# Scan on the vector engine, gates among the value steps, lag kernels before the indexer tile, column quarters and key turns within the value tiles

## What is computed

```
P = rms_norm(h) @ w_in       # u_s5 512 | q 512 | k 512 | v 512 | q_idx 256, k_idx 32, w_idx 8 | gate_s5, gate_att 1024 each
# branch S5: 32 groups of 16 channels, 64 complex states per group
s_t = a * s_(t-1) + B u_t    # diagonal, complex, over the sequence
y   = Re(C s_t) + D u_t      # then GELU and a GLU
# branch DSA
I[t,s] = sum_h w[t,h] relu(q_idx[t,h] . k_idx[s])
keep the top k (128 of the prompt, 256 of the past of a sample); softmax attention over them,
with a relative bias; the samples read k and v from a paged cache by a page table
h = h + (sigmoid(gate_s5) * S5 + sigmoid(gate_att) * DSA) @ w_out
```

## Time and profile before

| | us |
|---|---|
| median of 3 runs (1504.95 to 1506.29) | 1506.16 |
| the profiled execution, its own time | 1504.8 |
| its span | 1503.1 |
| busy: PE / DVE / ACT / POOL | 1425.5 / 609.4 / 451.4 / 262.3 |
| granted clock of PE, mean | 0.979 |

### The profile page before, as it was taken

How to read it: one execution, slowest core, us unless ns; L and a number is a source line. 1 busy time by engine, 2 the same in 40 slices (tenths; PEclk the granted TensorE clock), 3 DMA queues, 4 the chain that set the end, 5 groups by cost and what they waited for, 6 DMA issues and landing times. The chain is left out here.

```text
span 1503.1 us, 27575 instructions
## 1 busy us (share of the span) xinstructions
PE 1425.5 (95%) x10734; PEld 1294.4 (86%) x10734; DVE 609.4 (41%) x957; ACT 451.4 (30%) x647; POOL 262.3 (17%) x458
## 2 busy tenths in 40 slices
PE   6999999999999989989999897989999999999996
PEld 5999999999977767767777774848999999999996
DVE  4333233434452267506666321205543443344344
ACT  4332222222330320145555331202332212221234
POOL 4000000487002109701134313110000000000000
PEclk8999999999998999999999999999999999999998
DMA  8522332232222472153211658661233223322221
GB/s 135 153 84 77 87 89 84 85 90 86 63 56 34 99 115 60 24 137 75 57 57 57 196 179 300 195 224 42 84 88 94 85 84 87 95 85 84 83 71 60
DMA packets 228746, 148.05 MB, mean 98 GB/s; under 512 B 29729, under 2 KB 211817, under 8 KB 228666
## 3 DMA queue, kind: packets, MB, share of 16 engines
q1 hardware_dynamic: 195904, 118.06, 27.1%
q0 software_dynamic: 7088, 19.65, 5.3%
q10 hardware_dynamic: 25674, 9.25, 3.4%
HBM read 139.62 MB, written 6.12 MB: 97 GB/s over the span
## 5 line engine op out<-in xcount | busy, mean ns | idle before, releaser
L1614 DVE TENSOR_TENSOR w_low<-wraw,w_high 128x1024 fp32r<-128x1024 f32 x144 | 180.4, 1254 | 318.8 <-ACT w_high L1141 318.8
L575 PE MATMUL ps<-hn_high,w_high 128*128 128x272 f32 x1408 | 292.4, 289 | 2.9 <-DVE w_low L1614 2.9
L575 PE MATMUL ps<-hn_high,w_low 128*128 128x272 f32 x1408 | 292.4, 289 | 0.0
L575 PE MATMUL ps<-hn_low,w_high 128*128 128x272 f32 x1408 | 291.3, 288 | 0.0
L1141 ACT ACTIVATE w_high<-wraw 128x1024 fp32r<-128x1024 f32 x144 | 152.5, 1060 | 443.0 <-PE ps L575 437.9
L575 PEld LDWEIGHTS ps<-hn_high,w_high 128*128 128x128 f32 x1408 | 222.4, 189 | 3.1 <-issue 3.0
L575 PEld LDWEIGHTS ps<-hn_low,w_high 128*128 128x128 f32 x1408 | 222.2, 189 | 0.0
L575 PEld LDWEIGHTS ps<-hn_high,w_low 128*128 128x128 f32 x1408 | 220.7, 190 | 0.0
L575 PE MATMUL ps<-act_high,w_high 128*128 128x272 f32 x832 | 173.1, 289 | 3.0 <-DVE act_low L1614 1.8
L575 PE MATMUL ps<-act_high,w_low 128*128 128x272 f32 x832 | 172.2, 288 | 0.0
L575 PE MATMUL ps<-act_low,w_high 128*128 128x272 f32 x832 | 171.6, 288 | 0.0
(11 more groups left out here) (328 smaller groups left out, 1591.8 us busy)
## 6 DMA issues: line engine op xcount, KB each, us to landing
wraw<-in_w_ffn_in SPq DMA_DIRECT2D x88, 512.0 KB, 3.9
wraw<-in_w_ffn_out SPq DMA_DIRECT2D x32, 512.0 KB, 4.0
wslot<-in_w_in SPq DMA_DIRECT2D x16, 512.0 KB, 4.0
wraw<-in_w_ffn_out SPq DMA_DIRECT2D x16, 384.0 KB, 3.4
wslot<-in_w_in SPq DMA_DIRECT2D x4, 1024.0 KB, 6.4
wslot<-in_cache_k POOLq DMA_DIRECT2D x16, 256.0 KB, 4.6
wslot<-in_w_s_glu SPq DMA_DIRECT2D x16, 256.0 KB, 3.1
wslot<-in_cache_k SPq DMA_DIRECT2D x16, 256.0 KB, 4.4
```

Source lines behind the costliest of these rows:

```text
L575: ins = pe.matmul(ps[:, bank + h, 0:HALF], a[:, w_at, k, :], x[:, lo_at(k) if x is x_lo else k, h * HALF:(h + 1) * HALF], start=(k == 0 an ...
L1614: return dve.tensor_tensor(o, a, b, op)
```

## The change

- The lag kernels go before the indexer tile, in one round over eight places of the array (64 rows by 32 columns each); ACT copies them out in 16 pieces (`kpair`), POOL adds D before its transfers.
- The 32 sample tokens of the indexer, k and v tiles are done in column quarters (`sample_cols`): per block k four matmuls of 64 columns at four column places instead of one of 256. The copies out of them are in four pieces too.
- The 12 transfers of `uch` are issued by SP between the loads of q tile 1 and 2, not by ACT after q tile 1; `kidx` is written out earlier.
- The chunk inputs alternate the two column halves.
- The scan goes from POOL to the DVE, between the weighted sums and the first top-k pass. The third pass (512 keys) goes round by round into 16 of the first 24 steps of prompt attention, `qbd` behind the samples' page copies.
- The keys are turned within the two value tiles; value tile 0 waits for the evacuation of key tile 1.
- Gate halves: per group one after key step 4, two after the last score, five after value steps 1 to 5.
- The loads of the first key pages 1 and 2 wait for `tbm_done` 28 and 32 instead of all biased scores; `fin_t` and the 512-key scores swap their memory.

```diff
-        GA_AFTER_K, GA_AFTER_V = (2, 3, 5, 6), (4, 5)
+        GA_AFTER_K, GA_AFTER_V = (4,), (1, 2, 3, 4, 5)
...
# SP
-            load("q", (0, rows("w_in"), C_Q, P))
+            load("q", (0, rows("w_in"), C_Q, P), hi=1)
+            sp.wait_ge(s["u_out"], 16 * 8)
+            sp.wait_ge(s["u_zero"], 1)
+            for k in range(CH):
+                sp.dma_start(uch[16 * k:16 * k + 16, :, 0:NC], scr_u[k].rearrange("q (g c) n -> c (q g) n", c=GC)).then_inc(s["u_in"], 16)
...
+            load("q", (0, rows("w_in"), C_Q, P), lo=1)
+            load("kv", (0, rows("w_in"), C_K, 256))
...
# PE, behind the turned input matrices
+            pe.wait_ge(s["input_mats_out"], 6)
+            for r in range(4):
+                for c, y in enumerate((yre, yim)):
+                    for q in range(4):
+                        gp = 4 * r + q
+                        for h in range(2):
+                            sl = slice(64 * h, 64 * h + 64)
+                            ins = pe.matmul(ps[32 * q:32 * q + 16, 4 + h, P * r:P * r + P], bbar[sl, c, gp, :], y[sl, gp, 0:CH, :],
+                                            start=(r == 0 and c == 0), stop=(c == 1), skip_group_check=True, tile_position=(64 * h, 32 * q))
+            ins.then_inc(s["lag_kernels"], 1)
...
+            def sample_cols(bank, cols_of):
+
+                for k in range(DK):
+                    for c in range(4):
+                        ins = pe.matmul(ps[32 * c:32 * c + 32, bank, 0:64], hn[:, k, SEQ:NT], cols_of(k, c), start=(k == 0), stop=(k == DK - 1),
+                                        skip_group_check=True, tile_position=(0, 32 * c))
+                return ins
...
             def kv_body(i, slot, n, ready):
                 pe.wait_ge(w_ready[slot], ready)
                 pe.wait_ge(s["evac"], n + (EV0 - 1))
+                if i == 2:
+                    pe.wait_ge(s["evac"], n + EV0)
...
+                    if i >= 2 and tt % 2:
+                        turn_keys(2 * i - 4 + tt // 2)
+                sample_cols(4 * slot + 2, lambda k, c: w[:, k, 64 * c:64 * c + 64]).then_inc(s["mm_done"], 1)
...
# DVE
+            dve.wait_ge(s["chunk_inputs_out"], 4)
+            link(dve.memset(vst[:, :, :, 0:1], 0.0))
+            vb = vst[:, :, :, 1:1 + NC].rearrange("p c g (b j) -> p c g b j", j=8)
+            for j in range(1, 8):
+                advance([vb[:, c, :, :, j] for c in range(2)], [vb[:, c, :, :, j - 1] for c in range(2)],
+                        [cpow[:, 1, c, :].unsqueeze(2).broadcast_to([P, GP, 8]) for c in range(2)], (GP, 8))
...
+                if qb < 3:
+                    top(sc[qb], TOPK_P // 8)
+                    select(qb)
...
+                    top_round(scs)
+                    if x < 24 and x % 3 < 2:
+                        top_round(sc[3])
+                    if x == 22:
+                        select(3)
```

More of the change, by code:

```diff
@@ L737, in idx_body @@
                     acc(ps[0:m, b + 2, 40 * tt:40 * tt + 40], [(hn[:, k, tok_out(tt)], w[:, k, 256:296]) for k in range(DK)])
-                acc(ps[0:32, b + 3, 0:256], [(hn[:, k, SEQ:NT], w[:, k, 0:256]) for k in range(DK)])
+                sample_cols(b + 3, lambda k, c: w[:, k, 64 * c:64 * c + 64])
                 acc(ps[0:8, b + 3, 256:288], [(w[:, k, 288:296], hn[:, k, SEQ:NT]) for k in range(DK)]).then_inc(s["mm_done"], 1)
             tiles(pe, "idx", idx_body)
[L742 to L753, removed]
+            pe.wait_ge(s["lag_kernels_out"], 2)
             pe.wait_ge(s["evac"], EV0 + first_tile["u"])
@@ L804, in _ @@
                     gp = 4 * q + g4
-                    for h in range(2):
-                        for c in range(2):
+                    for c in range(2):
+                        for h in range(2):
                             ins = pe.matmul(ps[64 * h:64 * h + 64, 2 * q + c, UC * g4:UC * g4 + UC], gb[:, c, gp, 64 * h:64 * h + 64],
@@ L810, in _, with turn_keys @@
             pe.wait_ge(s["chunk_inputs_out"], 4)
+            def turn_keys(j):
+                if j:
+                    pe.wait_ge(s["keys_out"], j)
+                for tt in range(5):
+                    m = P if tt < 4 else 32
+                    dst = ps[:, 3, P * tt:P * tt + P] if tt < 4 else ps[:, 7, 0:32]
+                    ins = pe.transpose(dst, ktok[0:m, tt, P * j:P * j + P], ident[0:m, 0:m])
+                ins.then_inc(s["keys_turned"], 1)
             def kv_body(i, slot, n, ready):
@@ L1266, in _ @@
                 act_e.activation(gb[:, r // 4, 4 * (r % 4):4 * (r % 4) + 4, :].rearrange("p g n -> p (g n)"), ps[:, (r + 2) % 8, :], ACT.Copy).then_inc(s["input_mats_out"], 1)
+            act_e.wait_ge(s["lag_kernels"], 1)
+            for half in range(2):
+                for q in range(4):
+                    for h in range(2):
+                        ins = act_e.activation(kpair[half][:, :, q, h, :], ps[32 * q:32 * q + 16, 4 + h, 256 * half:256 * half + 256]
+                                               .rearrange("p (r n) -> p r n", r=2), ACT.Copy)
+                ins.then_inc(s["lag_kernels_out"], 1)
             def relus(qb, half):
@@ L1295, in _ @@
                     relus(3, i)
[L1296 to L1302, removed]
             for q in range(4):
@@ L1314, in _ @@
                     kidx_page(act_e, NB * NPAGE - ACT_PAGES * (4 - i) + k)
+                for j in range(2 * i - 4, 2 * i - 2) if i >= 2 else ():
+                    act_e.wait_ge(s["keys_turned"], j + 1)
+                    act_e.activation(kT[:, j, 0:SEQ], ps[:, 3, :], ACT.Copy)
+                    act_e.activation(kT[:, j, SEQ:NT], ps[:, 7, 0:32], ACT.Copy).then_inc(s["keys_out"], 1)
                 act_e.wait_ge(s["mm_done"], MM0 + n + 1)
@@ L1435, in _ @@
                 act_e.activation(ptS[0:32, 8, :], ps[0:32, 5, 0:P], ACT.Copy).then_inc(s["sample_probs_out"], 1)
-                ga_out(8 * g + 6)
-                ga_out(8 * g + 7)
+                for m in range(len(GA_AFTER_V)):
+                    ga_out(8 * g + GA_K + 2 + m)
             act_e.wait_ge(s["sample_att_turned"], 1)
@@ L1849, in _ @@
                 dve.wait_ge(s["relu_done"], x + 1)
+                if x == 16:
+                    dve.wait_ge(s["kidx_out"], 32)
                 if h == 0:
@@ L1874, in _ @@
+            dve.sem_inc(s["scan_done"], 1)
             dve.wait_ge(s["sample_const_in"], 16 * 12)
```

159 lines of the change are left out of this document (71 added, 88 removed).

## The result

| | before | changed |
|---|---|---|
| median, us | 1506.19 (1504.95 to 1506.84, 6 runs) | 1492.06 (1488.11 to 1495.99, 6 runs) |
| ratio | | 0.9912, 95% 0.9901 to 0.9923 |
| profiled execution, own time / span | 1504.8 / 1503.1 | 1490.67 / 1488.9 |
| granted clock, mean | 0.979 | 0.973 |

A forecast was written before the change was run, and what follows sets the result against it. PE was taken as the bound, holding 40% of the span in the chain of waits. Terms A to F summed to -19 us from 1504.8, so 1485.8, given as 1486.5 because the runs' median is 1.4 higher; range 1474 to 1499.

The forecast's parts named there:

- A: Lag kernels ahead of the indexer tile, its sample part in quarters, idle and lower clock before the key turns: -5.75 us.
- B: `uch` through SP's queue: new wait of 5.0 before q tile 2, none before the chunk inputs; sum -0.2 us.
- they are in by about 532: The twelve `uch` transfers on SP, free to go at about 516, would all have landed by about 532.
- C: k and v tiles: quartered sample matmuls -8.5, new wait at value tile 0 +1.5, end waits -0.4; sum -7.4 us.
- D: Scan on the DVE takes 46 us, so PE waits for the DVE before the head weights: +6 us.
- rival 1: The scan on the DVE runs at the packed rate, so D is 0: about 1480 (25%).
- E: Prompt attention: 16 third-pass rounds fit the DVE's free time in the first 24 steps: +0.3 us.
- F: Gate halves among the value steps: `cache_v` waits and their lower clock go, short key-step waits come: -12 us.
- all of it goes: At the first value buffer's refill, the wait and the lower clock behind it both vanish: about 8 us per group.
- (4): SP held up: q tile 2 comes 4 us later still, 1490 (8%).
- (3): Quarter matmuls run one after another: +11 on PE, 6 given back by D's wait, 1491 (5%).
- (2): Moved gates gain nothing, since key steps become what waits for pages: F is 0, 1498 (8%).

The follow-up runs named there:

- experiment 5: Changed kernel with the 12 `uch` transfers issued by ACT behind q tile 1 again: ratio 0.9924 to the kernel before, median 1493.23 us.
- experiment 6: Changed kernel with the k and v tiles' sample tokens again as whole 256-column matmuls: ratio 0.9910 to the kernel before, median 1491.91 us.
- experiment 12: Changed kernel with waits covered, first top-k pass before the scan, 12 kidx pages earlier, k and v tiles whole: 0.9851 of the kernel before, 1483.66 us.
- experiment 4: Changed kernel with the scan back on POOL, third top-k pass left in the attention steps: ratio 0.9883 to the kernel before, median 1488.46 us.
- experiment 3: Changed kernel with the first top-k pass moved ahead of the scan on the DVE: ratio 0.9899 to the kernel before, median 1487.96 us.
- 2: Changed kernel with the gate halves back in their old places: ratio 0.9940 to the kernel before, median 1495.19 us.
- 7: Kernel before with only the gate halves moved: ratio 0.9964 to the kernel before, median 1501.07 us.
- experiment 11: Changed kernel with waits covered, first top-k pass before the scan, 12 kidx pages earlier, gate halves in old places: 0.9867 of the kernel before, 1484.27 us.
- Experiment 10: Changed kernel with waits covered, first top-k pass before the scan, 12 kidx pages earlier, gate halves after value steps 1, 2, 3, 5, 7: 0.9788, 1474.66 us.

## Why the prediction was right, and where it was wrong

**A, right in sum, its sizes off.** Lag kernels: 1.9 for 2.4. The indexer tile shrank by 4.4 and not 2.1. From 459 to 469 the kernel before ran it at granted clock 0.50, which I had not looked at: the whole matmuls (466.9 to 471.5) cost 4.6 there and not 3.5, so the quarters save 2.8. Another 2.1 are the matmuls of 40 columns, where the lower clock began at 459 before and at 462.7 after, and 0.5 went back on the last ones; for that part the quarters are not the cause, and it was luck. The idle was 4.5 for 4.1. Its lower clock cost 2.8 (key turns to u tile 1: 12.2 against 9.4), not 1.6. In sum A came out 1.1 better, since these misses partly cancel.

**B, right in time, its parts not.** "A new wait of 5.0, between 1 and 8" was 2.2. The step that failed is "they are in by about 532": the last was issued at 524.9 and had landed 3.2 later, at 528.1. The weights, issued at 526.13, were there at 530.2, about 2 behind it, as forecast. By the Trainium skill (DMA: Bandwidth & Descriptors, Queues, rings and completion order) one ring takes its descriptors in order. The rows fit that but do not test it, since loads of this size (512 KB) take 4.0 from issue to landing here (median of four). Undoing B costs 0 to 2 us (experiment 5), within the noise.

**C, right on PE, not as a gain in time.** -7.0 for -7.4, with quarters at 1.03 from start to start and not 1.4, and 1.7 of lower clock behind the wait before value tile 0 that I had not counted. What I had not seen is that C's gain did not show in the kernel's time: undone in the changed kernel it cost nothing that could be measured (experiment 6), undone with the waits covered 0.6 to 2.8 (experiment 12). In the changed kernel part of it went into the wait for the DVE.

**D, right in sum, by luck: +6.1 for +6**, and 4.4 to 6.0 by experiment 4 (experiment 3, 2.0 to 3.6, is not clear of the noise). Both parts moved: the scan took 44.3 and not 46 and started 3 us earlier, so the wait was 3.9 and not 6; the lower clock behind it (646 to 661, turns of 1.11 for 0.66), which I had not counted, made up for that. The four products of 128 elements took 1.25, not 0.93, the packed pair 0.49 (0.53) and the pair that writes the state 0.68: steps do cost, here in the ratio of 0.68 to 0.49. The packed rate of rival 1 is out. The rule I took from the Trainium skill (VectorE: DVE Perf Modes, The DRAIN you can't avoid) gave 44 for a packed scan, which is the sum measured, but by coincidence: a pair took 0.49 where one such operation takes 0.29, so the two overlap. I had left out that section's exception, that a next operation which isn't held starts earlier; the rows agree with that.

**E, right**: 164.52 us for the attention steps in both kernels, though the DVE carries 16 more rounds; the 0.3 came one step behind them.

**F, wrong in size: -5.5 in the profile, -2.6 to -5.4 by three experiments (2, 7, 11), for -12.** The step that failed is "all of it goes", where "it" holds 0.9 and 1.9 at the lower clock besides the 5.13 of wait. The waits did go (9.7), and the six waits of 0.5 came (3.0): -6.7, as worked out. But 5.6 of the 12 was the cost of the lower clock, charged to the wait, and that did not go: with the wait gone the clock fell at the end of each group, and the first turns (3.39 for 1.97) and the start of the output projection (3.4 longer) ran at the lower clock in its place. That is 4.8 of the 6.5 missed; about 1 more is that each of the six moved gate halves costs some 0.2 more among the value steps. Experiment 10 also has a gate half behind the last value step, and against the old places (experiment 11) it is 11.9 faster by ratio: the size that F promised, from other places than F had.

So the forecast time was 5.6 too low. In the profiles the terms miss by 4.9: F by 6.5 and the ends by 1.1 one way, A and B together by 3.3 the other way, C, D and E by 0.5. That the time lies so near is in part luck, since F's miss is half cancelled. Of the rivals, (4) at 1490 and (3) at 1491 were the nearest in time, and neither happened: q tile 2 waited 2.2 and not 9, and the quarters took 1.03. Of (2), gates moved for nothing, no wait for `cache_k` appeared.

## What to carry to other kernels

Price a wait of the tensor engine and the lower clock behind it apart. Here the clock's part did not come back when the wait alone went (experiments 2 and 7); in experiment 10, with a gate half at the place where the clock fell next, the lower clock was gone from the profile and the time fell by more than the waits. Look at each engine's finishing time at the place where they meet, not only the latest one: here the DVE and SP's page loads stood 4.5 us apart, and the gain on PE uncovered the second. A faster engine is no gain for work that was not late: the scan was 26 us quicker on the DVE and the kernel 4 to 6 us slower for it.

## What the runs showed that I had not expected

- The granted clock falls to 0.50 with PE busy and no wait near. In the kernel before it does so at 459, in the matmuls of 40 columns, 17 us after PE's last wait (windows of the indexer tile; 11 records in a us at 1.00, 6 at 0.50):

```profile
457.00:458.00 1.00, 1.00 (x11) 1.00 (x11) 0.00 (x0) 0.00 (x0) 0.00 (x0) 1.00 0.00 0
...
460.00:461.00 1.00, 1.00 (x6) 1.00 (x7) 0.00 (x0) 0.00 (x0) 0.00 (x0) 0.50 0.00 0
```

 The Trainium skill (TensorE: Matmul & The Clock Gate, Part 1: The HAM clock gate) ties the clock to how busy the engine has been; these rows don't bear that out as they stand, since PE is busy through all of both windows.
- The same program has its low stretches at other places and in other number from run to run: 55 and 75 us in two profiles, 6.3 us of time apart. The changed kernel's 12 runs spread over 8.9 us, the 37 of the kernel before over 4.0 but for one at 1510.34, so a gain of 3 us needs many runs to be seen here.
- 64 matmuls of 128 columns at eight places of the array took 1.93 us from start to start, 30 ns each, against 68 with four places and twice the rows.
